# 192 turns of the identity on TensorE ahead of the scores against the cached keys

## The reference

```
q_lat  = einsum('bshd,chd->bshc', q_nope, w_uk)
s_past = (einsum('bshc,btc->bhst', q_lat, lat_past)
          + einsum('bshr,btr->bhst', q_rope, kr_past)) * SOFTMAX_SCALE
s_new  = (einsum('bshc,btc->bhst', q_lat, lat)
          + einsum('bshr,btr->bhst', q_rope, k_rope)) * SOFTMAX_SCALE
p      = softmax(concatenate([s_past, where(causal, s_new, NEG_INF)]))
o_lat  = p[..., :T] @ lat_past + p[..., T:] @ lat
o      = einsum('bshc,chd->bshd', o_lat, w_uv)
```

## Time and profile before

| | |
|---|---|
| median of 3 runs | 1480.25 us (1477.3 to 1482.81) |
| profiled execution | 1478.69 us |
| its span, first to last instruction | 1476.9 us |
| mean granted clock of TensorE | 0.976 of full speed |
| PE busy | 1404.9 us (95%) |
| DVE, ACT, POOL busy | 690.4, 396.9, 374.5 us |

### The profile page before, as it was taken

The page is one execution under the profiler, slowest core; times in us unless marked ns, Lnnn a source line. Parts: engine busy times, 40 slices in busy tenths (PEclk is TensorE's granted clock), DMA queues, the critical chain, the costliest instruction groups (busy, mean ns, idle before and its releaser), DMA issues.

```text
span 1476.9 us, 25516 instructions
## 1 busy us (share of the span) xinstructions
PE 1404.9 (95%) x10814; PEld 1281.4 (87%) x10814; DVE 690.4 (47%) x1358; ACT 396.9 (27%) x875; POOL 374.5 (25%) x278
## 2 busy tenths in 40 slices
PE   6999999999669998999999999999999999999998
PEld 4899776666456765899999999999999999999997
DVE  4846655665627765666632232332323323223245
ACT  5521655555302332322401202102011020110244
POOL 0032042323301213502241605206043060240400
PEclk8999999999969999999999999999999999999999
DMA  9612234244644755600020302103012030020103
GB/s 348 249 51 59 97 96 149 83 136 162 203 143 165 250 179 184 212 10 29 29 86 3 112 1 65 50 1 101 15 45 71 1 100 15 29 86 1 43 8 115
DMA packets 94177, 139.66 MB, mean 95 GB/s; under 512 B 14283, under 2 KB 65431, under 8 KB 89831
## 3 DMA queue, kind: packets, MB, share of 16 engines
q1 hardware_dynamic: 83957, 95.74, 19.8%
q0 software_dynamic: 5760, 37.75, 7.4%
q10 hardware_dynamic: 4346, 4.54, 0.9%
HBM read 121.98 MB, written 13.79 MB: 92 GB/s over the span
## 4 chain that ended last, share of the span: by engine, by line
PE 87%; DMA 4%; DVE 4%; issue 2%; SPq 2%; ACT 1%; POOL 0%; DVEq 0%; ACTq 0%
PE psa L1254 26%; PE psa L1268 25%; PE psa L1232 6%; PE psa L792 4%; PE psa L1126 4%; PE psa L858 3%; PE psa L1176 3%; PE psa L974 3%; PE psa L1012 2%; DMA wm<-in_w_mod 2%; PE psa L995 2%; SPq L524 1%; DMA qd<-q_f 1%; PE psa L873 1%; PE psa L395 1%
## 5 line engine op out<-in xcount | busy, mean ns | idle before, releaser
L1254 PE MATMUL psa<-hhi,wr 128*128 128x384 f32 (+1 forms) x1536 | 374.6, 327 | 0.0
L1254 PEld LDWEIGHTS psa<-hhi,wr 128*128 128x128 f32 x1536 | 270.8, 188 | 0.1
L1268 PE MATMUL psa<-g_hi,wd_hi 128*128 128x384 f32 (+1 forms) x768 | 251.6, 328 | 0.0
L1254 PE MATMUL psa<-hlo,wr 128*128 128x384 f32 (+1 forms) x768 | 250.6, 326 | 0.0
L1268 PE MATMUL psa<-g_hi,wd_lo 128*128 128x384 f32 (+1 forms) x768 | 250.6, 326 | 0.0
L1268 PE MATMUL psa<-g_lo,wd_hi 128*128 128x384 f32 (+1 forms) x768 | 250.5, 326 | 0.0
L2175 DVE SCALAR_TENSOR_TENSOR xT<-psa,modT,xT 128x384 f32<-128x384 f32 (+1 forms) x216 | 123.2, 571 | 190.7 <-PE psa L1268 160.6
L1694 ACT ACTIVATE g_relu<-psa 128x384 f32<-128x384 f32 (+1 forms) x96 | 45.4, 473 | 600.9 <-PE psa L1254 600.9
L587 POOL TENSOR_SCALAR wr<-wraw 128x1024 fp32r<-128x1024 f32 x34 | 36.4, 1070 | 567.8 <-PE psa L1254 490.2
L2239 DVE TENSOR_TENSOR psa<-psa,g_relu 128x384 f32<-128x384 f32 (+1 forms) x96 | 52.2, 544 | 261.6 <-ACT g_relu L1694 261.6
L1254 PEld LDWEIGHTS psa<-hlo,wr 128*128 128x128 f32 x768 | 144.2, 188 | 0.1
(11 more groups left out here) (305 smaller groups left out, 2254.4 us busy)
## 6 DMA issues: line engine op xcount, KB each, us to landing
wmod<-in_w_mod SPq DMA_DIRECT2D x8, 2048.0 KB, 8.2
wraw<-in_w_up SPq DMA_DIRECT2D x32, 512.0 KB, 4.0
wraw<-in_w_down SPq DMA_DIRECT2D x32, 512.0 KB, 3.5
wm<-in_w_mod SPq DMA_DIRECT2D x4, 2048.0 KB, 19.5
x_scr<-xT SPq DMA_DIRECT2D x1, 4352.0 KB, 19.4
wraw<-in_w_out SPq DMA_DIRECT2D x8, 512.0 KB, 4.1
out_y_p<-yst SPq DMA_DIRECT2D x8, 512.0 KB, 2.7
xstage<-in_x_prompt SPq DMA_DIRECT2D x3, 1024.0 KB, 11.1
```

What stands on the lines that cost most here:

```text
L1254: mm = pe.matmul(out[:, :N], w[:, c * P:c * P + P], x[:, c, c0:c0 + N], start=(c == 0 and q == 0), stop=(c == KD - 1 and q == 2))
L1268: mm = pe.matmul(out[:, :N], w[:, c, n * P:n * P + P], x[:, c, c0:c0 + N], start=(c == 0 and q == 0), stop=(c == FG - 1 and q == 2))
```

## The change

Ahead of the first key scores TensorE waits for the last exponential of the prompt's attention, then turns the 128x128 identity 192 times into the four quarters of bank 7 in rotation, with no semaphore raised. Nothing reads what it writes. All else is as it was; lines behind it move down by three.

```diff
             mm.then_inc(sem("oT_mm"), 1)
 
+        pe.wait_ge(sem("exp"), NT)
+        for k in range(192):
+            pe.transpose(bank(7)[:, P * (k % 4):P * (k % 4) + P], ident[:, :], ident[:, :])
         key_scores(0)
         key_scores(1)
         new_scores()
```

## The result

The changed kernel takes 1488.3 us (median; 1486.37 to 1491.38) beside 1480.14 us of the kernel before (1477.3 to 1482.81): ratio 1.0062, 95% interval 1.0046 to 1.0078. It is slower by 8 us, above the range of the prediction. Its profiled execution has a span of 1484.6 us, 7.7 us more than before.

What follows compares the result with a forecast made beforehand. TensorE, busy 95% of the span, bounds the kernel; at this place a DMA transfer ends last. Wait 0, hidden turns 0, gain 0.4 us: 1480.25 to 1479.9 us on the median; range 1475.5 to 1483.5 us.

Steps and rivals of the forecast that it cites:

- The wait: TensorE's wait for the last softmax exponential ahead of the turns: no new wait, costs nothing.
- The turns were hidden: Ahead of the first scores: 192 turns take 21.9 us, covered by the 25.22 us wait for the query copies.
- They held the clock: During the turns: they count as activity, so the clock stays at 2.4 GHz from 394 to 416 us.
- the second rival: Turns do not hold the clock, end 11.6 us after the copies land; 1491.9 us, chance 0.07.
- The remainder: Idle time between the turns' end and the copies' landing: 3.4 us, likeliest to lose the clock.
- 0.4 taken: Gain at the first scores, taken near the lower end of 0 to 3.3 us.
- the first rival's gain: Clock kept to the end of the wait, first scores at full rate: 1.79 to 3.3 us gained, chance 0.25.
- DVE, ACT and POOL see nothing of it: Turns into bank 7: nobody reads them, no semaphore is raised, so the landing at 419.37 us does not move.
- The part on instructions: 384 more TensorE instructions to fetch during the turns: only a stall over 3.4 us would show, taken as nothing.
- what TensorE gains stays gained: Behind the place, TensorE is busy 83.00 of 83.00 us from 457 to 540 us, so a gain reaches the end.
- a difference that arises after 450 us, where I expect none: Sign that the forecast is wrong: a time difference arising later in the kernel, behind the place of the change.
- a stall of 3 us: Third rival: turns stall on fetching or bank 7's port and end 0 to 3 us late; 1482 us, chance 0.06.

Runs made afterwards that it cites:

- the later splits: Changed kernel (192 turns) in which POOL turns 384 columns of the fourth and sixth W_out parts into their high half twice: 1484.14 us, ratio 1.0021.
- the wait on POOL: POOL's fifth and later W_out splits wait for the last normalised output: on kernel before 1478.94 us, on changed kernel 1480.96 us, with 224 turns 1479.12 us.

## Why the prediction was wrong

*Right.* The wait cost nothing. The turns were hidden: 21.18 us by the trace, 21.9 forecast, a spacing of 0.109 us against 0.113. They held the clock, against the rule of the Trainium skill (TensorE: Matmul & The Clock Gate, section Part 4: PE-mode transpose) that the prediction weighs; the second rival fell. The remainder was 5.97 us and not 3.4, for the most part because in this profile the turns began at 392.50 us and not at 394.15. It took the clock, and there was no gain at the place (0.4 taken; the first scores took 0.6 us longer). With 224 turns the first rival's gain came as priced, 2.0 us in 1.79 to 3.3.

*Wrong, first: "DVE, ACT and POOL see nothing of it".* POOL and DVE saw the length of the program, through loads of W_out 180 us later. The part on instructions took nothing because "only a stall longer than the 3.4 us that are over would show". It asked whether fetching would stall the turns, and had no term for what a longer program shifts elsewhere. That term measured 4.2 us by the phase alone (the later splits against the changed kernel), of 6.0 us in all beside the kernel before on the same chip (1482.38 to 1488.38). The remaining 2 us (1.8 between the later splits and the kernel before, 2.0 between the two kernels with the wait on POOL) are not traced to a cause.

*Wrong, second: "what TensorE gains stays gained", and "a difference that arises after 450 us, where I expect none".* The witness was the stretch from 457 to 540 us, where TensorE never waits. Even there a gain did not stay: with 224 turns and the wait on POOL, 1.7 of the 2 us went between 466 and 544 us. And the trace of before had another witness behind it: at 604.05 and 605.36 us TensorE waits for hlo, and the five steps that make hlo take 7.97 us where one such step takes 0.56 us at 590.85 us. Read for slack, those rows say that this stretch has none, and that DVE's length there may depend on POOL, which is busy beside it; that half a microsecond of POOL's phase tips it, the later splits show. No change of TensorE's instructions could be called free before that was priced. The range upward, 1483.5 us, held a stall of 3 us and no such shift.

The Trainium skill (SBUF — State Buffer, section Who interferes with whom) states a rule that could have led there: between a DVE copy in a two-port mode and GpSimd, whichever issues first keeps the shared ports for the whole instruction, and a DVE step with two inputs in SBUF contends with a GpSimd step that reads SBUF. The runs agree: 0.17 against 2.22 us for the copy, 2.43 against 7.97 to 10.15 us for five subtractions, while the reductions beside them kept their 0.15 us. The Trainium skill says of instruction fetching (Runtime: NRT & Kernel Launch, section Instruction fetch mechanics) that crossing a 16 KB border is mostly hidden. By the place of the stalls, TensorE stood still at one border for 1.13 to 2.12 us in six profiles and crossed the same one without a stall in others; stalls at other borders stayed under 1 us.

## What to carry to other kernels

Work that is hidden is not free if it is on an engine's instruction stream: look for the stretches behind it in which two engines meet with no slack (short DVE steps beside POOL's long ones, and TensorE waiting for them), and ask what half a microsecond either way does there. Where one is found, mend that first: one wait on POOL was worth 3.3 us in the kernel before and 7.4 us in the changed one. Keeping the clock, 2.0 us at its place, is not shown to pay even with it: 1479.12 us with 224 turns, 1478.94 us without any, on one chip. A single profile of a kernel can be a lucky one (11.10 against 12.72 us and 20.69 against 22.72 us here); profile it twice before a difference of two traces is put down to a change.

## What the runs showed of the hardware

- With one more 16 KB packet of TensorE instructions, 512 KB loads of W_out land in 3.6 instead of 4.1 or 4.2 us, in every kernel that leaves POOL's work as before; where POOL's work was moved they took 4.2 us with 86 packets, 3.6 to 4.0 us with 87 and 3.8 us with 88. Loads of the next weights (w_up) stay at 4.0 or 4.1 us. Why is open.
- An idle time of 1.98 us behind 24.67 us of turns left the clock at 1.00, one of 5.97 us behind 21.18 us of turns lost it before the copies landed; at W_out waits of 0.89, 0.53 and 1.84 us in a row lost it, 1.52 with 0.53 us kept it, and of two profiles of the kernel before, one lost it behind 1.07 and 0.52 us and the other kept it behind 1.06 and 0.52 us.
- A 64x4 copy on DVE took 0.17 us with POOL idle, 0.89 or 0.90 us when it began within a POOL step of 1.31 to 1.41 us, and 2.22 us within one of 2.54 us; each of these ended within 0.04 us of the end of POOL's step.
